# Head-norm sums from two rounded parts of the squares, and a rank-16 product with its weight parts side by side

## The chip, the cores and the metric

The kernel runs on one core of one Trainium2 chip. The metric is device time in microseconds from launch to end. A core has TensorE (PE: matrix products into PSUM; its weight loads are PEld), VectorE (DVE), ScalarE (ACT), GpSimd (POOL) and SyncE (SP), which issues most of the transfers. Each engine works through its own list in order; the lists are tied by semaphores only.

## The reference

One decoder layer on x (512 tokens, 1024 channels), float32: a gated feed-forward block, a mixing block, a second feed-forward block, a last norm. Only the mixing block matters here:

```python
proj = h @ w_in_mix          # hq hf hi hg | gq gk gv gg | g_low (16 columns) | r_hg r_gla
gk   = g_low @ w_gk_up + b_gk_up                       # rank 16 -> 256 decay logits
o    = chunked_gated_linear_attention(q, k, v, log_a)  # 4 HGRN2 heads, 4 GLA heads, 128 channels each
o    = rms_norm(o, norm_gain) * silu(g)                # per head: x * rsqrt(mean(x*x) + 1e-6) * gain
merged = sigmoid(r_hg) * (y_hg @ w_up_hg) + sigmoid(r_gla) * (y_gla @ w_up_gla)
```

## The kernel before

Activations lie with channels on the 128 partitions and the 512 tokens along the free axis. A large product is made from numbers in a rounded 32-bit format (fp32r), of which one pass of 512 columns goes through TensorE at a time. To keep float32 accuracy each operand is split into a high part (rounded) and a low part (the rest), and three passes are summed: high weight by high activation (L575), high by low (L576), low by high (L577). Weights come in units: 1024 rows by 256 columns in RAW; ScalarE writes the high part WH (L1127, `split_hi`), VectorE the low part WL (L1649, `split_lo`). Two slots alternate. The two "v" kinds are made the other way round, tokens out, in passes of 256 columns (L620 to L622).

The mixing block has 15 units, MIX: hf hq vh gh hf hq vh gh low gk gq vg gg vg gg, numbered 0 to 14. Unit 8, "low", has 16 columns. Each unit has 8 steps on TensorE, and the list STAGES_AT puts attention work between the steps: for each of 8 heads three groups of scores (`score_levels`, L898, L903, L904), the far scores (`score_far`, L913 to L921), the output (`head_out`, L934, into PSUM bank 7), and the norm sum (`head_norm`, L942). Head 0 has its norm at step 39, head 1 at 51, head 2 at 70 (inside "low", steps 64 to 71), head 3 at 89. The scores of head 1 start at step 41, of head 2 at 60, of head 3 at 78, of head 5 at 104.

ScalarE and VectorE follow one written list, ORDER: "... V0 A0 E3 a1 Q0 b1 T0 E4 U0 V1 A1 Q1 E5 T1 a2 U1 b2 E6 V2 A2 E7 Q2 a3 T2 b3 U2 E8 V3 G0 G1 A3 E9 Q3 a4 T3 E10 b4 ... E12 Q4 V5 A5 a5 ...". For a head or preparation j:

- E: ScalarE converts the next unit's high part and moves unit j out of PSUM; VectorE makes the next low part.
- a, b: decays and preparation of the score operands. VectorE runs a cumulative sum (L2092), GpSimd forms differences from it (L544 to L556), ScalarE takes exponentials, VectorE multiplies (L2114, L2115, L2120, L2123). The first scores of the head need the second L2123.
- V, A: VectorE and ScalarE copy scores out of PSUM (V: L2157, L2170).
- Q: ScalarE squares the head's output (L1522, in `squares`), one operation of 128x512 that raises sq_o; VectorE multiplies output by gate (L2176, in `gate_out`) and raises og_done. `head_norm` on TensorE waits for both and sums the squares over the 128 partitions with a matrix of ones, in float32.
- T, U: inverse root and gain (L1529, L1531, L2182), then high and low part of the result (L1535, L2186).

The rank-16 code is copied to S and multiplied by w_gk_up (GKW, 16 rows) in float32 (`gk_up`, L951, step 80).

Of the kernel before, what the change touches and what calls it, by code (L numbers as in the profile page):

```python
# [23 lines left out]
def trunk_program(nc, x, c, w_ada, b_ada, norm_gains, ffn1_w_in, ffn1_w_down, w_in_mix, w_gk_up, b_gk_up,  # L24
                  lb_logits, hg_norm, gla_norm, w_up_hg, w_up_gla, w_out, ffn2_w_in, ffn2_w_down,
                  final_norm, out):
    F32, F32R, BF16, I8 = mybir.dt.float32, mybir.dt.float32r, mybir.dt.bfloat16, mybir.dt.int8
    ACT, ALU = mybir.ActivationFunctionType, mybir.AluOpType
    ds = bass.ds

    P = 128
    T = x.shape[1]
    D = x.shape[2]
    DB = D // P
# [3 lines left out]
    CW = 256  # L38
# [3 lines left out]
    HEADS = 4  # L42
# [15 lines left out]
    N_MIX = N_F1DOWN + 11  # L58
# [7 lines left out]
    mix_at = {}  # L66
    for j, (kind, _, half) in enumerate(MIX):
        mix_at[kind, half] = j
    RANK = 16
# [3 lines left out]
    with ctx:  # L73
        def sb(name, shape, dt=F32):
            return ctx.enter_context(nc.sbuf_tensor(name, shape, dt))

        def sem(name):
            return ctx.enter_context(nc.semaphore(name))
# [5 lines left out]
        S = sb("S", [P, T])  # L84
# [18 lines left out]
        LBD = sb("LBD", [P, HEADS])  # L103
        GT = sb("GT", [P, 2, NC])
        FT = sb("FT", [P, 2, NC])
        GKW = sb("GKW", [RANK, 256])

        H_BYTES = DB * T * 4
        ARENA = 106496
# [3 lines left out]
        def place(name, shape, offset, dt=F32):  # L113
            return nc.alloc_sbuf_tensor_at(name, shape, dt, offset=base + offset)
# [54 lines left out]
        W512 = place("W512", [P, T], 104448)  # L169
        YH = [place("YHh", [P, HEADS, T], 8192, F32R), place("YHg", [P, HEADS, T], 0, F32R)]  # L170
        YL = [place("YLh", [P, HEADS, T], 16384, F32R), place("YLg", [P, HEADS, T], 24576, F32R)]
        MH = place("MH", [P, DB, T], 53248, F32R)
        ML = place("ML", [P, DB, T], 69632, F32R)
        RG = [place(f"RG{s}", [P, 2, T], 86016 + 4096 * s) for s in range(2)]
# [55 lines left out]
        near_done, evac_v = sem("near_done"), sem("evac_v")  # L230
        evac_a = sem("evac_a")
        pv_done = sem("pv_done")
        sq_o, og_done = sem("sq_o"), sem("og_done")
        n_done, rs_ln, rs_ready = sem("n_done"), sem("rs_ln"), sem("rs_ready")
        yf_ready, y_hi, y_lo = sem("yf_ready"), sem("y_hi"), sem("y_lo")

# [23 lines left out]
        def slot(n):  # L260
            return n % 2
# [27 lines left out]
        def norm_in(a):  # L289

            if a < HEADS:
                return CHG[:, a, :], KHG[:, a, :]
            return QHG[:, a - HEADS, :], VHG[:, a - HEADS, :]
# [50 lines left out]

        def ada_buffer(piece, j):
            return ADAW[1 if piece >= LATE_PIECE else 0][j]

        def mix_banks(j):
            return (2, 3) if j % 2 == 0 else (0, 1)
# [215 lines left out]
        def _(pe):  # L565
# [13 lines left out]
            def unit(n, value, banks, ahi, alo, kb0=0, nk=DB, first=True, last=True, wait_h=None,  # L579
                     width=CW, before=None):  # L580

                pe.wait_ge(unit_lo, value)
                whi, wlo = weights(n, width)
                for k in range(nk):
                    if before is not None:
                        before(k)
                    if wait_h is not None:
                        pe.wait_ge(h_lo, wait_h + k + 1)
                    for m in range(max(width // P, 1)):
                        w = slice(m * P, min((m + 1) * P, width))  # L590
                        rows = w.stop - w.start
                        ins = three(PS[0:rows, banks[m], :], whi[:, k, w], wlo[:, k, w], ahi[:, kb0 + k, :],
                                    alo[:, kb0 + k, :], first and k == 0, last and k == nk - 1)
                ins.then_inc(unit_done, 1)

            def unit_x(n, value, banks, ahi, alo, kb0=0, nk=DB, first=True, before=None):
# [13 lines left out]
            def unit_v(n, banks, before):  # L610

                pe.wait_ge(unit_lo, n + 1)
                whi, wlo = weights(n)
                for t in range(TT):
                    ps = PS[:, banks[t // 2], (t % 2) * CW:(t % 2 + 1) * CW]
                    tok = slice(t * P, (t + 1) * P)
                    for k in range(DB):
                        if k % 4 == 0:
                            before(2 * t + k // 4)
                        mm(ps, HH[:, k, tok], whi[:, k, :], start=k == 0, stop=False)  # L620
                        mm(ps, HL[:, k, tok], whi[:, k, :], start=False, stop=False)  # L621
                        ins = mm(ps, HH[:, k, tok], wlo[:, k, :], start=False, stop=k == DB - 1)  # L622
                ins.then_inc(unit_done, 1)
# [314 lines left out]
            def head_norm(a):  # L938

                pe.wait_ge(sq_o, a + 1)  # L940
                pe.wait_ge(og_done, a + 1)
                mm(PS[:, 7, :], ONES[:, :], norm_in(a)[0], start=True, stop=True).then_inc(n_done, 1)  # L942

            def gk_up():

                pe.wait_ge(gkw_in, 16)
                pe.wait_ge(mix_evac, mix_at["low", 0] + 1)
                pe.wait_ge(evac_a, 2 * HEADS - 3)
                pe.wait_ge(rs_ln, HEADS - 1)
                for g in range(2):  # L950
                    ins = mm(PS[:, 6 + g, :], GKW[:, g * P:(g + 1) * P], S[0:RANK, :], start=True, stop=True)  # L951
                ins.then_inc(gk_mm, 1)

            def stages_at(step):
# [24 lines left out]
            for j in range(2, len(MIX)):  # L979
                n = N_MIX + j  # L980
                kind = MIX[j][0]
                pe.wait_ge(mix_evac, j - 1)
                if kind in ("vh", "vg"):
                    unit_v(n, mix_banks(j), lambda k: stages_at(8 * j + k))
                else:
                    unit(n, n + 1, mix_banks(j), HH, HL, width=RANK if kind == "low" else CW, before=lambda k: stages_at(8 * j + k))


            def late_reduce(pair, b):
# [119 lines left out]
        def _(act):  # L1109
# [7 lines left out]

            for dst, src in small:
                act.dma_start(dst, src).then_inc(small_in, 16)
            act.dma_start(GKW[:, :], w_gk_up[0]).then_inc(gkw_in, 16)  # L1120

            def split_hi(n, raw_val, done_val=None, size=UNIT):

                act.wait_ge(raw_in[slot(n)], raw_val)
                if done_val is not None:
                    act.wait_ge(unit_done, done_val)
                A(WH[slot(n)][:, 0:size], RAW[slot(n)][:, 0:size], ACT.Copy).then_inc(unit_hi, 1)  # L1127

            def down_size(piece):
                return (UNIT, UNIT, (FB - 16) * CW)[piece]  # L1130
# [313 lines left out]
            def evacuate(j):  # L1444
                if MIX[j][0] in ("hf", "hq", "gh", "gg"):
                    tables[0] = "sigmoid or silu"
                n = N_MIX + j
                kind, _, half = MIX[j]
                act.wait_ge(unit_done, n + 1)
                ps = PS[:, mix_banks(j)[0]:mix_banks(j)[0] + 2, :]  # L1450
                two = slice(2 * half, 2 * half + 2)
                toks = ps.rearrange("p b (t c) -> p (b t) c", c=CW)
                if kind == "hf":
                    A(CHG[:, two, :], ps, ACT.Sigmoid)
                    A(KHG[:, two, :], ps, ACT.Sigmoid, scale=-1.0).then_inc(mix_evac, 1)
                elif kind == "hq":
                    A(QHG[:, two, :], ps, ACT.Silu).then_inc(mix_evac, 1)
                elif kind == "vh":
                    A(VHG[:, :, half * CW:(half + 1) * CW], toks, ACT.Copy).then_inc(mix_evac, 1)
                elif kind == "vg":  # L1460
                    A(VGL[:, :, half * CW:(half + 1) * CW], toks, ACT.Copy).then_inc(mix_evac, 1)
                elif kind == "gh":
                    A(GO[:, two, :], ps, ACT.Silu).then_inc(mix_evac, 1)
                elif kind == "gg":
                    A(GO[:, HEADS + 2 * half:HEADS + 2 * half + 2, :], ps, ACT.Silu).then_inc(mix_evac, 1)
                elif kind == "low":
                    A(S[0:RANK, :], PS[0:RANK, mix_banks(j)[0], :], ACT.Copy).then_inc(mix_evac, 1)
                elif kind == "gk":
                    A(KGL[:, :, :], ps, ACT.Copy).then_inc(mix_evac, 1)
                elif kind == "gq":  # L1470
                    A(QGL[:, :, :], ps, ACT.Copy, scale=64.0 ** -0.5).then_inc(mix_evac, 1)
# [47 lines left out]

            def squares(a):  # L1520
                act.wait_ge(pv_done, a + 1)
                A(norm_in(a)[0], PS[:, 7, :], ACT.Square).then_inc(sq_o, 1)  # L1522

            def inverse_rms(a):

# [107 lines left out]
        def _(dve):  # L1633
# [9 lines left out]
            def split_lo(n, value, done_val=None, size=UNIT):  # L1643

                if done_val is not None:
                    dve.wait_ge(unit_done, done_val)
                dve.wait_ge(unit_hi, value)
                s = slot(n)
                V.tensor_tensor(WL[s][:, 0:size], RAW[s][:, 0:size], WH[s][:, 0:size].bitcast(F32), ALU.subtract)\  # L1649
                    .then_inc(unit_lo, 1)  # L1650

# [520 lines left out]

            def gate_out(a):
                dve.wait_ge(sq_o, a + 1)
                dve.wait_ge(mix_evac, G_NEEDS[a])
                V.tensor_tensor(GO[:, a, :], GO[:, a, :], PS[:, 7, :], ALU.mult).then_inc(og_done, 1)  # L2176

# [172 lines left out]
```

## Time and profile before

| | |
|---|---|
| median of 3 runs | 1189.76 us (1188.7 to 1189.96) |
| profiled execution: its own time | 1188.77 us |
| its span, first to last instruction | 1186.9 us |
| granted TensorE clock, mean over the span | 0.992 |
| instructions | 18541 |
| DVE L1649 (low parts of weights) | 55 operations, 120.5 us |
| ACT L1127 (high parts of weights) | 55 operations, 100.5 us |
| DMA moved, mean | 143.51 MB, 121 GB/s |

Times in rows are microseconds from the span's start unless marked ns. A timeline row is start, duration, engine, line, operation, output<-input, shape, and in brackets the engine's idle time before it and what ended that. A matmul's shown duration includes its way through the pipeline, so the cost of one pass in a stream is read from start to start. PEclk is the granted clock as a share of full speed.

### The profile page before, as it was taken

What the parts mean: (1) busy time and instruction counts of PE and PEld (TensorE: products, weight loads), DVE (VectorE), ACT (ScalarE), POOL (GpSimd) and SP (SyncE); (2) the same over time, 40 slices, a digit from 0 to 9 for tenths busy, and PEclk for the clock granted to TensorE, in tenths of its full rate; (3) what the DMA queues carried; (4) which work ended last, traced back from release to release, by engine and by line L of the source; (5) the groups of instructions that cost most, each with busy time, mean ns of one, the idle gap of its engine ahead of it and who ended that gap; (6) DMA issues with size and microseconds to landing.
All of it is one profiled execution on the core that took longest, in us unless ns stands there. A gap on an engine that the chain in (4) does not pass through costs nothing.

```text
span 1186.9 us, 18541 instructions
## 1 busy us (share of the span) xinstructions
PE 1158.7 (98%) x7385; PEld 1039.3 (88%) x7385; DVE 781.7 (66%) x1061; ACT 507.5 (43%) x646; POOL 90.7 (8%) x137
## 2 busy tenths in 40 slices
PE   5999999999999999999999999999999999999997
PEld 5789999998889997877887888888999999998887
DVE  5788888767777677566463446755868887863222
ACT  6455554452222466555344322234455544452322
POOL 2000000002220122222010001000000000000000
PEclk8899999999999999999999999999999999999999
DMA  9433333337885131122221457442223333332211
GB/s 353 147 104 108 106 106 106 106 97 264 306 288 179 37 102 44 36 71 72 71 72 36 142 178 245 145 142 72 72 71 107 106 106 106 106 97 98 98 63 71
DMA packets 115126, 143.51 MB, mean 121 GB/s; under 512 B 4084, under 2 KB 102784, under 8 KB 115072
## 3 DMA queue, kind: packets, MB, share of 16 engines
q1 hardware_dynamic: 106800, 113.32, 29.2%
q0 software_dynamic: 8064, 29.36, 7.0%
q8 instruction: 37, 0.61, 0.2%
q14 instruction: 17, 0.14, 0.0%
q10 hardware_dynamic: 208, 0.08, 0.0%
HBM read 140.65 MB, written 2.10 MB: 120 GB/s over the span
## 4 chain that ended last, share of the span: by engine, by line
PE 87%; DVE 7%; ACT 4%; issue 1%; DMA 1%; SPq 0%; DVEq 0%; ACTq 0%
PE PS L819 29%; PE PS L575 16%; PE PS L577 15%; PE PS L576 15%; PE PS L898 1%; PE PS L934 1%; PE PS L620 1%; PE PS L904 1%; PE PS L621 1%; PE PS L622 1%; PE PS L733 1%; DVE ACC L1751 1%; DMA ADA<-in_w_ada_dram 1%; DVE ACC0a L1762 1%; ACT WH L1127 1%
## 5 line engine op out<-in xcount | busy, mean ns | idle before, releaser
L1649 DVE TENSOR_TENSOR WL<-RAW,WH 128x2048 fp32r<-128x2048 f32 (+2 forms) x55 | 120.5, 2191 | 129.4 <-ACT WH L1127 129.3
L575 PE MATMUL PS<-HH,WH 128*128 128x512 f32 (+2 forms) x488 | 186.1, 381 | 4.4 <-DVE HL L1677 3.0
L1127 ACT ACTIVATE WH<-RAW 128x2048 fp32r<-128x2048 f32 (+2 forms) x55 | 100.5, 1828 | 194.3 <-PE PS L577 187.7
L577 PE MATMUL PS<-HH,WL 128*128 128x512 f32 (+2 forms) x488 | 177.8, 364 | 0.0
L576 PE MATMUL PS<-HL,WH 128*128 128x512 f32 (+2 forms) x488 | 177.7, 364 | 0.0
L819 PE MATMUL PS<-HH,WH 128*128 128x256 f32 x576 | 163.3, 284 | 0.3
L819 PE MATMUL PS<-HL,WH 128*128 128x256 f32 x576 | 163.0, 283 | 0.0
L819 PE MATMUL PS<-HH,WL 128*128 128x256 f32 x576 | 163.0, 283 | 0.0
L575 PE MATMUL PS<-UH,WH 128*128 128x512 f32 (+1 forms) x416 | 147.0, 353 | 0.0
L577 PE MATMUL PS<-UH,WL 128*128 128x512 f32 (+1 forms) x416 | 145.8, 351 | 0.0
L576 PE MATMUL PS<-UL,WH 128*128 128x512 f32 (+1 forms) x416 | 145.8, 350 | 0.0
L819 PE MATMUL PS<-TH,WH 128*128 128x256 f32 x432 | 122.3, 283 | 0.0
L819 PE MATMUL PS<-TL,WH 128*128 128x256 f32 x432 | 122.3, 283 | 0.0
L819 PE MATMUL PS<-TH,WL 128*128 128x256 f32 x432 | 122.2, 283 | 0.0
L575 PEld LDWEIGHTS PS<-HH,WH 128*128 128x128 f32 (+1 forms) x488 | 91.9, 188 | 24.8 <-issue 6.7
L1930 DVE TENSOR_TENSOR WL<-SW,WH 128x1024 fp32r<-128x1024 f32 x72 | 88.2, 1225 | 35.3 <-ACT WH L1310 35.2
L819 PEld LDWEIGHTS PS<-HH,WH 128*128 128x128 f32 x576 | 110.5, 192 | 0.8 <-DVE WL L1936 0.7
L819 PEld LDWEIGHTS PS<-HL,WH 128*128 128x128 f32 x576 | 110.6, 192 | 0.1
L819 PEld LDWEIGHTS PS<-HH,WL 128*128 128x128 f32 x576 | 110.5, 192 | 0.0
L577 PEld LDWEIGHTS PS<-HH,WL 128*128 128x128 f32 (+1 forms) x488 | 92.0, 188 | 15.8
L576 PEld LDWEIGHTS PS<-HL,WH 128*128 128x128 f32 (+1 forms) x488 | 92.2, 189 | 14.3 <-issue 1.1
L1310 ACT ACTIVATE WH<-SW 128x1024 fp32r<-128x1024 f32 x72 | 76.2, 1058 | 66.7 <-PE PS L819 63.8
(320 smaller groups left out, 2244.3 us busy)
## 6 DMA issues: line engine op xcount, KB each, us to landing
RAW<-in_ffn_w_in_dram SPq DMA_DIRECT2D x42, 1024.0 KB, 5.1
ADAW<-in_w_ada_dram POOLq DMA_DIRECT2D x56, 512.0 KB, 5.6
RAW<-in_w_in_mix_dram SPq DMA_DIRECT2D x22, 1024.0 KB, 5.3
RAW<-in_ffn_w_down_dram SPq DMA_DIRECT2D x16, 1024.0 KB, 5.1
ADA<-in_w_ada_dram SPq DMA_DIRECT2D x16, 512.0 KB, 10.5
RAW<-in_ffn_w_down_dram SPq DMA_DIRECT2D x7, 768.0 KB, 4.5
RAW<-in_w_out_dram SPq DMA_DIRECT2D x3, 1024.0 KB, 5.1
XST<-in_x_dram SPq DMA_DIRECT2D x4, 512.0 KB, 5.3
```

The lines of the kernel that those rows point to most:

```text
L575: mm(ps, whi, ahi, start=start, stop=False)
L576: mm(ps, whi, alo, start=False, stop=False)
L577: return mm(ps, wlo, ahi, start=False, stop=stop)
L620: mm(ps, HH[:, k, tok], whi[:, k, :], start=k == 0, stop=False)
L621: mm(ps, HL[:, k, tok], whi[:, k, :], start=False, stop=False)
L622: ins = mm(ps, HH[:, k, tok], wlo[:, k, :], start=False, stop=k == DB - 1)
L733: ins = mm(PS[:, 6, m:m + 1], ACC[:, m * P:(m + 1) * P], ONES[:, 0:1], start=True, stop=True)
L819: ins = mm(PS[:, bank, ROW], wt, at_tokens[:, k, :], start=start and k == 0 and j == 0, stop=k == 3 and j == 2, skip_group_check=True)
L1127: A(WH[slot(n)][:, 0:size], RAW[slot(n)][:, 0:size], ACT.Copy).then_inc(unit_hi, 1)
L1310: A(WH[tile][:, 8 * P * (1 - j):8 * P * (2 - j)], SW[:, 2 * j:2 * j + 2, :].rearrange("p s c -> p (s c)"), ACT.Copy).then_inc(op_hi, 1)
L1649: V.tensor_tensor(WL[s][:, 0:size], RAW[s][:, 0:size], WH[s][:, 0:size].bitcast(F32), ALU.subtract)\
L1930: V.tensor_tensor(WL[tile][:, w], SW[:, 2 * j:2 * j + 2, :].rearrange("p s c -> p (s c)"), WH[tile][:, w].bitcast(F32), ALU.subtract).then ...
```

## The change

The squares of each head are written twice by ScalarE, once in full and once rounded (SQH). VectorE subtracts to get the low part (SQL), ahead of the gate product. TensorE sums both rounded parts with the ones read as fp32r: two fp32r passes where there was one float32 product. SQL of the HGRN2 heads overwrites the full squares in place.

For unit "low" the two weight parts (16 columns each) lie side by side in WH, so that one pass multiplies both: 8 steps with two passes each (all 32 weight columns by HH, then by HL) in place of 8 with three. The 32 output rows go to S, and GKW holds w_gk_up twice, one copy below the other, so that `gk_up` adds the two halves.

```diff
-        GKW = sb("GKW", [RANK, 256])
+        GKW = sb("GKW", [2 * RANK, 256])
+        SQH = [place("SQHh", [P, HEADS, T], 16384, F32R), place("SQHg", [P, HEADS, T], 0, F32R)]
+        SQL = [place("SQLh", [P, HEADS, T], 8192, F32R), place("SQLg", [P, HEADS, T], 24576, F32R)]
...
+        def side_by_side(n):
+            both = WH[slot(n)][:, 0:2 * DB * RANK].rearrange("p (k c) -> p k c", c=2 * RANK)
+            return both[:, :, 0:RANK], both[:, :, RANK:2 * RANK], both
...
+            def low_unit(n, bank, before):
+                pe.wait_ge(unit_lo, n + 1)
+                both = side_by_side(n)[2]
+                for k in range(DB):
+                    before(k)
+                    mm(PS[0:2 * RANK, bank, :], both[:, k, :], HH[:, k, :], start=k == 0, stop=False)
+                    ins = mm(PS[0:2 * RANK, bank, :], both[:, k, :], HL[:, k, :], start=False, stop=k == DB - 1)
+                ins.then_inc(unit_done, 1)
...
             def head_norm(a):
                 pe.wait_ge(sq_o, a + 1)
+                pe.wait_ge(sq_lo, a + 1)
                 pe.wait_ge(og_done, a + 1)
-                mm(PS[:, 7, :], ONES[:, :], norm_in(a)[0], start=True, stop=True).then_inc(n_done, 1)
+                ones = ONES[:, :].bitcast(F32R)
+                mm(PS[:, 7, :], ones, SQH[a // HEADS][:, a % HEADS, :], start=True, stop=False)
+                mm(PS[:, 7, :], ones, SQL[a // HEADS][:, a % HEADS, :], start=False, stop=True).then_inc(n_done, 1)
...
-                pe.wait_ge(gkw_in, 16)
+                pe.wait_ge(gkw_in, 32)
...
-                    ins = mm(PS[:, 6 + g, :], GKW[:, g * P:(g + 1) * P], S[0:RANK, :], start=True, stop=True)
+                    ins = mm(PS[:, 6 + g, :], GKW[:, g * P:(g + 1) * P], S[0:2 * RANK, :], start=True, stop=True)
...
-            act.dma_start(GKW[:, :], w_gk_up[0]).then_inc(gkw_in, 16)
+            for part in range(2):
+                act.dma_start(GKW[RANK * part:RANK * (part + 1), :], w_gk_up[0]).then_inc(gkw_in, 16)
...
-                    A(S[0:RANK, :], PS[0:RANK, mix_banks(j)[0], :], ACT.Copy).then_inc(mix_evac, 1)
+                    A(S[0:2 * RANK, :], PS[0:2 * RANK, mix_banks(j)[0], :], ACT.Copy).then_inc(mix_evac, 1)
...
             def squares(a):
                 act.wait_ge(pv_done, a + 1)
-                A(norm_in(a)[0], PS[:, 7, :], ACT.Square).then_inc(sq_o, 1)
+                A(norm_in(a)[1], PS[:, 7, :], ACT.Square)
+                A(SQH[a // HEADS][:, a % HEADS, :], PS[:, 7, :], ACT.Square).then_inc(sq_o, 1)
...
             def gate_out(a):
                 dve.wait_ge(sq_o, a + 1)
+                V.tensor_tensor(SQL[a // HEADS][:, a % HEADS, :], norm_in(a)[1], SQH[a // HEADS][:, a % HEADS, :].bitcast(F32),
+                                ALU.subtract).then_inc(sq_lo, 1)
                 dve.wait_ge(mix_evac, G_NEEDS[a])
                 V.tensor_tensor(GO[:, a, :], GO[:, a, :], PS[:, 7, :], ALU.mult).then_inc(og_done, 1)
```

`split_hi` and `split_lo` of unit "low" write the two halves of `side_by_side`, 128 values per partition each as before.

## Rows read from the trace of the kernel before

**Rows 1.** the page: busy time by engine; the chain that ended last.

```profile
PE 1158.7 (98%) x7385; PEld 1039.3 (88%) x7385; DVE 781.7 (66%) x1061; ACT 507.5 (43%) x646; POOL 90.7 (8%) x137
...
PE 87%; DVE 7%; ACT 4%; issue 1%; DMA 1%; SPq 0%; DVEq 0%; ACTq 0%
```

**Rows 2.** windows: stretch, its us, PE PEld DVE ACT POOL busy, PEclk, DMA, GB/s.

```profile
440.00:670.00 230.00, 227.74 (x1237) 182.01 (x1236) 130.53 (x232) 111.70 (x156) 34.88 (x44) 1.00 0.22 69
40.00:54.00 14.00, 13.13 (x54) 10.41 (x54) 7.82 (x12) 5.59 (x7) 0.00 (x0) 0.76 0.46 152
```

**Rows 3.** waits of TensorE, mixing stage: total us, times, longest.

```profile
PE PS L898 <- DVE KP L2123: 1.0, 3, 0.6
PE PS L951 <- issue: 0.6, 1, 0.6
PE PS L942 <- DVE GO L2176: 0.5, 1, 0.5
```

**Rows 4.** groups, mixing stage: count | busy us, mean ns | idle before.

```profile
L575 PE MATMUL PS<-HH,WH 128*16 128x512 f32 x8 | 3.6, 456 | 0.0
```

**Rows 5.** timeline, TensorE, around head 2: start, duration (us), instruction, count.

```profile
519.28 1.02 PE L942 MATMUL PS<-CHG,ONES 128*128 128x512 f32 x2
...
520.36 0.40 PE L576 MATMUL PS<-HL,WH 128*16 128x512 f32 x1
...
521.06 0.39 PE L576 MATMUL PS<-HL,WH 128*16 128x512 f32 x1
```

**Rows 6.** timeline, all engines, around head 0.

```profile
459.75 0.69 DVE L2176 TENSOR_TENSOR GO<-GO,PS 128x512 f32<-128x512 f32 x1 [0.77 <-ACT CHG L1522]
...
460.36 0.87 DVE L2114 TENSOR_TENSOR QU<-QU,QHG 128x512 f32<-128x512 f32 x1
...
460.59 1.10 PE L942 MATMUL PS<-CHG,ONES 128*128 128x512 f32 x2 [0.48 <-DVE GO L2176]
460.64 1.48 POOL L553 TENSOR_TENSOR KP<-CHG 128x512 f32<-128x512 f32 x1
...
461.15 1.52 DVE L2115 TENSOR_TENSOR KL<-KL,KHG 128x512 f32<-128x512 f32 x1
...
464.14 0.41 DVE L2123 TENSOR_TENSOR KP<-KP,KHG 128x256 f32<-128x256 f32 x1
...
464.61 0.55 PE L898 MATMUL PS<-QP,KP 128*128 128x64 f32 x3 [0.18 <-DVE KP L2123]
```

**Rows 7.** timeline, ScalarE, around head 1.

```profile
482.85 0.60 ACT L1522 ACTIVATE CHG<-PS 128x512 f32<-128x512 f32 x1 [4.32 <-PE PS L934]
483.34 1.91 ACT L1127 ACTIVATE WH<-RAW 128x2048 fp32r<-128x2048 f32 x1
```

**Rows 8.** timeline, ScalarE and VectorE, around head 2.

```profile
517.35 0.59 ACT L1522 ACTIVATE CHG<-PS 128x512 f32<-128x512 f32 x1
...
517.97 0.69 DVE L2176 TENSOR_TENSOR GO<-GO,PS 128x512 f32<-128x512 f32 x1 [0.46 <-ACT CHG L1522]
...
520.10 1.23 DVE L2092 TENSOR_TENSOR_SCAN CHG<-RST,CHG 128x512 f32<-128x512 bf16 x1 [1.04 <-ACT CHG L1483]
```

**Rows 9.** timeline, VectorE and TensorE, head 4.

```profile
593.25 0.69 DVE L2176 TENSOR_TENSOR GO<-GO,PS 128x512 f32<-128x512 f32 x1 [0.46 <-ACT QHG L1522]
593.85 0.91 DVE L2157 COPY_PREDICATED SC<-MASK,PS 128x256 f32<-128x256 int8 x2
...
594.91 0.29 PE L903 MATMUL PS<-QP,KP 64*128 64x64 f32 x1
```

**Rows 10.** timeline, VectorE and TensorE, heads 3 and 7.

```profile
553.33 0.69 DVE L2176 TENSOR_TENSOR GO<-GO,PS 128x512 f32<-128x512 f32 x1 [0.71 <-ACT CHG L1522]
...
556.68 1.02 PE L942 MATMUL PS<-CHG,ONES 128*128 128x512 f32 x2
...
655.48 0.68 DVE L2176 TENSOR_TENSOR GO<-GO,PS 128x512 f32<-128x512 f32 x1
...
657.27 0.59 PE L942 MATMUL PS<-QHG,ONES 128*128 128x512 f32 x1
```

More of the change, by code:

```diff
@@ L232, in trunk_program @@
         pv_done = sem("pv_done")
-        sq_o, og_done = sem("sq_o"), sem("og_done")
+        sq_o, sq_lo, og_done = sem("sq_o"), sem("sq_lo"), sem("og_done")
         n_done, rs_ln, rs_ready = sem("n_done"), sem("rs_ln"), sem("rs_ready")
@@ L984, in _ @@
                     unit_v(n, mix_banks(j), lambda k: stages_at(8 * j + k))
+                elif kind == "low":
+                    low_unit(n, mix_banks(j)[0], lambda k: stages_at(8 * j + k))
                 else:
-                    unit(n, n + 1, mix_banks(j), HH, HL, width=RANK if kind == "low" else CW, before=lambda k: stages_at(8 * j + k))
+                    unit(n, n + 1, mix_banks(j), HH, HL, before=lambda k: stages_at(8 * j + k))
             def late_reduce(pair, b):
@@ L1126, in split_hi @@
                     act.wait_ge(unit_done, done_val)
-                A(WH[slot(n)][:, 0:size], RAW[slot(n)][:, 0:size], ACT.Copy).then_inc(unit_hi, 1)
+                if n == N_MIX + mix_at["low", 0]:
+                    A(side_by_side(n)[0], RAW[slot(n)][:, 0:size].rearrange("p (k c) -> p k c", c=RANK), ACT.Copy).then_inc(unit_hi, 1)
+                else:
+                    A(WH[slot(n)][:, 0:size], RAW[slot(n)][:, 0:size], ACT.Copy).then_inc(unit_hi, 1)
             def down_size(piece):
@@ L1648, in split_lo @@
                 s = slot(n)
+                if n == N_MIX + mix_at["low", 0]:
+                    hi, lo, _ = side_by_side(n)
+                    V.tensor_tensor(lo, RAW[s][:, 0:size].rearrange("p (k c) -> p k c", c=RANK), hi.bitcast(F32), ALU.subtract)\
+                        .then_inc(unit_lo, 1)
+                    return
                 V.tensor_tensor(WL[s][:, 0:size], RAW[s][:, 0:size], WH[s][:, 0:size].bitcast(F32), ALU.subtract)\
```

## The prediction

> **What bounds the kernel now.** I read the page first, for the busy shares and the chain that ended last: TensorE is busy for 98% of the span and carries 87% of the chain [rows 1]. Then the windows: in the mixing stage, 440 to 670 us, TensorE is busy 227.7 of 230 us at full clock, with VectorE at 130.5 and ScalarE at 111.7 [rows 2]. So a pass less on TensorE looks like time gained. But the change also lengthens the way over ScalarE and VectorE, and TensorE does wait for that way in a few places. So I read the waits of TensorE next [rows 3]: three times for the score operands (1.0 us in all), once 0.6 ahead of L951 (there the unit's low part is due, an L1649 that VectorE makes after the same score operands), once 0.5 for the gate product of a head. Each is small, but a wait above zero marks a place where TensorE is early: what TensorE saves ahead of it is lost in the wait, and what VectorE or ScalarE adds ahead of it is paid in full. So the sum is made piece by piece between these places, from the timelines.
>
> **What TensorE saves.** The float32 sum of a head is two passes [rows 5]. It starts at 519.28; the third matmul behind it (the second L576) starts at 521.06, four matmuls after its end, at a pace of (521.06 - 520.36)/3 = 0.233 each. So the sum costs 521.06 - 519.28 - 4 x 0.233 = 0.85 us. Two fp32r passes at 0.23 cost 0.46. Saved: 0.39 a head, 8 x 0.39 = 3.1 us. Unit "low" has 8 passes of each kind [rows 4], 24; 16 remain. A pass of 16 weight columns costs the same 0.233 as any [rows 5], so 32 columns cost no more: 8 x 0.233 = 1.9 us saved. Together 5.0 us, if all of it counted.
>
> **What ScalarE and VectorE add, per head.** One more square: 0.59 long, but the operation behind a square starts 0.49 after it [rows 7], so +0.5 on ScalarE, and sq_o rises 0.5 later. One more subtraction SQL on VectorE ahead of the gate product. No row shows it; its bounds are the gate product, same shape, 0.69 with a start-to-start of 0.61, and L2115, two SBUF inputs beside a GpSimd operation, 1.52 [rows 6]. GpSimd works at head 0 only (in the other pieces SQL falls into its pauses), so I take 0.6 start to start elsewhere. A head's gate product then ends 0.5 + 0.6 = 1.1 later.
>
> **Head 0.** The square ended at 459.73, GO ran 459.75 to 460.44, and TensorE, which had waited 0.48 us, started at 460.59, 0.15 after it [rows 6]. New: squares to 460.23; SQL ends by about 461.2 (nearest row: L2114 at 460.36, same shape and inputs, 0.87, beside the same GpSimd work); GO to 461.85; norm sum from 462.0, +1.4. It is 0.39 shorter, so TensorE goes on at +1.0. Before, it came to the next scores (L898, 464.61) with 0.18 idle; its last matmul had started at 464.04 by the modelled length of 0.39, so it could have started at 464.27. New: 465.3. VectorE's second L2123 ended at 464.55; it too moves, but less than GO, since L2115 now falls mostly behind GpSimd's work: about 465.2. TensorE is late by 465.3 - 464.6 = **+0.7**. With SQL at 0.69 it is +0.4, at 1.52 +1.2.
>
> The Trainium skill, "SBUF — State Buffer", section "Who interferes with whom", says that a VectorE operation with two SBUF inputs and a GpSimd operation that reads SBUF exclude each other for the whole instruction, and that one with a single SBUF input is free. The rows bear it out: GO, which reads PSUM, ran in 0.69 beside GpSimd, and L2115 ended just after L553 (462.12) by the time of one operation [rows 6]. By that rule SQL waits for the GpSimd operation under way and then blocks the next: +0.8 for the piece. Without the rule it would be +0.4.
>
> **Head 1.** The square (482.85, for which ScalarE had waited 4.32 us) stands directly ahead of the conversion L1127 [rows 7], of E5, T1, a2 and so of everything up to the scores of head 2 at step 60, where TensorE waits (one of the three waits in [rows 3]). +0.5 on ScalarE passes through. SQL is hidden: VectorE has nothing to do until the conversion of 1.91 us ends. TensorE's 0.39 at step 51 lies ahead of that wait and is lost. **+0.5**, bounds 0.4 and 0.6.
>
> **Head 2.** The same, towards the scores of head 3 at step 78. The squares begin at 517.35; VectorE's sum L2092 starts at 520.10 after an idle 1.04 behind the decay logarithm L1483 of ScalarE [rows 8]. SQL takes 0.6 more on VectorE against that idle 1.04, so only ScalarE's 0.5 counts: **+0.5** (0.4 to 0.6). At this norm TensorE waits for GO: 518.66 + 1.1 + 0.15 = 519.9, while it is there from 519.28 less six steps of "low" at one pass less, 1.4. Then it runs to step 78, and would be there early. It waits. So the 0.39 and the whole 1.9 us of unit "low" are lost: the waits at L898 and L951 [rows 3] only grow.
>
> **Heads 3 and 7.** At head 3 GO ends at 554.02 and TensorE comes at 556.68; at head 7 655.48 + 0.68 = 656.16 against 657.27 [rows 10]. A GO later by 1.1 is just in time in both; at head 7 SQL may start as soon as L1649 is through, so it is +0.6 there. Heads 4, 5 and 6 do not wait either (L942 waited once in eight [rows 3]). So each of heads 3 to 7 keeps its saving: 5 x 0.39 = **-2.0 us**; if one loses it, -1.6.
>
> **Head 4, the new place.** Behind its GO (593.25 to 593.94) VectorE runs the two L2157 of head 5's scores (593.85, 0.91 long), and 0.15 after them, at 594.91, TensorE starts L903 of the third group, which reuses their bank [rows 9]. That is a chain without slack: square + 0.5, SQL + 0.6. **+1.1** (0.6 to 1.3).
>
> **Edits at nothing.** The second w_gk_up transfer is one more issue on ScalarE's queue at the very start, beside a TensorE that waits for others; 32 rows in place of 16 for L951 and the copy to S change no column count. Strided conversions of "low" handle the same 128 values. If the cover went, each is some tenths.
>
> **Sum.** +0.7 + 0.5 + 0.5 + 1.1 - 2.0 = +0.8, with the 0.1 by the rule left aside. On the profiled execution (span 1186.9, 1188.77 in all) that is 1189.6; the median of the runs shown stands 0.99 above it, so 1190.6 in those terms. With all low bounds 0.4 + 0.4 + 0.4 + 0.6 - 2.0 = -0.2, with all high ones 1.2 + 0.6 + 0.6 + 1.3 - 1.6 = +2.1: the forecast's own range is 1189.6 to 1191.9. Below 0.2% (2.4 us) a measurement of this kernel does not tell a change from none, so the forecast is "same".
>
> **Rivals.**
>
> 1. The savings count. If the waits in [rows 3] are no more than jitter of an engine that is busy 98% [rows 1], the 5.0 us come through: 1184.7, faster. For it: 2.3 us idle in 230 [rows 2]. Against it: the idle stands where the lists cross, with a named releaser. Half-way, if ScalarE's 0.5 hides at heads 1 and 2 but the savings there still die, it is 1189.8, still same. Chance of the faster case 0.14.
> 2. SQL in front of the preparation. If SQL isn't hidden at heads 1 and 2, and at head 3, whose GO stands directly ahead of the next cumulative sum (L2092), reaches the scores of head 4, then 1.2 + 1.1 + 1.1 + 1.1 + 1.1 - 2.0 = +3.6: 1193.4, slower. It decides once the pieces add up to over 4.4 us against the 2.0 saved. Against it: the idle 1.04 in [rows 8] and the conversion of 1.91 in [rows 7]. Chance 0.09.
> 3. The clock. Near the start, 40 to 54 us, where TensorE had waited, the granted clock averaged 0.76 [rows 2], that is part of the time at 1.2 in place of 2.4 GHz, which cost 0.24 x 14 = 3.4 us. At head 0 the wait grows from 0.5 to 1.9 us. If the clock falls there: 1190.6 + 3.4 = 1194.0, slower. Against it: 1.00 throughout the stage, waits of 0.6 included. Chance 0.04.
> 4. It doesn't do what it says: a pass with the ones read as fp32r costs as much as a float32 one. Then the 2.0 are gone and head 0 pays 0.4 more: +3.2, 1193.0, slower. Against it: the same format in L576 at 0.233. Chance 0.05.
>
> **Chances.** The forecast 0.68, rival 1 0.14, rivals 2 to 4 0.18 together. Faster by over 0.2% 0.14; within 0.2% 0.69 (the forecast and the weak ends of the rivals); slower 0.17. Eight times in ten: 1187.0 to 1193.2.
>
> **What would show it.** L942 as two passes 0.23 apart, x16 in all. A wait of about 1.9 us at head 0's norm; the waits at L898 for heads 2 and 3 not smaller but larger, together by over 2 us; a new wait of about 1.3 us ahead of L903 in the third group of head 5; no wait at the norms of heads 3 to 7. L2092 of head 3 later against the end of unit 7 by 0.5. I am wrong if the wait at L898 for head 3 stays at its old size while unit "low" is 1.9 shorter (rival 1), if SQL shows over 1 us outside head 0 or delays an L2092 of heads 1 to 3 by more than 0.6 (rival 2), or if PEclk is below 1.00 anywhere in the stage (rival 3).

## The result

| | kernel before | changed kernel |
|---|---|---|
| median (runs) | 1189.64 us (17) | 1190.96 us (17) |
| lowest to highest | 1187.42 to 1190.22 | 1189.55 to 1192.37 |
| ratio, after to before | | 1.0016 (95% interval 1.0009 to 1.0024) |
| profiled execution, span | 1186.9 us | 1189.5 us |

The forecast was 1190.6, no change that can be told. The median is 0.4 us above it and inside the range; the time is longer by 0.16%, with an interval that reaches both sides of the 0.2% below which I called two times the same. The way there was as forecast in most of its waits and wrong in one term, the clock.

### The profile page after: what moved, and what is told of

Same layout as the page of the kernel before. It is cut to its first block, busy times and chain, and to the rows that moved or that the text cites. A ratio compares the mean times of both kernels' runs of the same rounds, so it can differ in the third digit from the quotient of the medians.

```text
span 1189.5 us, 18534 instructions
## 1 busy us (share of the span) xinstructions
PE 1156.6 (97%) x7377; PEld 1041.4 (88%) x7377; DVE 785.7 (66%) x1069; ACT 511.5 (43%) x654; POOL 90.5 (8%) x137
## 4 chain that ended last, share of the span: by engine, by line
PE 87%; DVE 6%; ACT 4%; issue 1%; DMA 0%; ACTq 0%; DVEq 0%
PE PS L836 29%; PE PS L582 16%; PE PS L584 16%; PE PS L583 16%; PE PS L915 1%; PE PS L951 1%; PE PS L921 1%; PE PS L637 1%; PE PS L638 1%; PE PS L639 1%; PE PS L750 1%; DVE ACC L1783 1%; ACT WH L1153 1%; PE PS L938 1%; DVE ACC0b L1794 1%
## 5 line engine op out<-in xcount | busy, mean ns | idle before, releaser
L1681 DVE TENSOR_TENSOR WL<-RAW,WH 128x2048 fp32r<-128x2048 f32 (+1 forms) x54 | 120.2, 2226 | 128.2 <-ACT WH L1153 128.1
L582 PE MATMUL PS<-HH,WH 128*128 128x512 f32 (+1 forms) x480 | 182.5, 380 | 4.5 <-DVE HL L1709 3.0
L1153 ACT ACTIVATE WH<-RAW 128x2048 fp32r<-128x2048 f32 (+1 forms) x54 | 100.2, 1856 | 194.5 <-PE PS L584 187.7
L584 PE MATMUL PS<-HH,WL 128*128 128x512 f32 (+1 forms) x480 | 175.6, 366 | 0.0
L583 PE MATMUL PS<-HL,WH 128*128 128x512 f32 (+1 forms) x480 | 175.6, 366 | 0.0
L582 PEld LDWEIGHTS PS<-HH,WH 128*128 128x128 f32 x480 | 92.0, 192 | 23.5 <-issue 5.8
L836 PEld LDWEIGHTS PS<-HH,WH 128*128 128x128 f32 x576 | 110.5, 192 | 0.8 <-DVE WL L1968 0.7
L836 PEld LDWEIGHTS PS<-HL,WH 128*128 128x128 f32 x576 | 110.6, 192 | 0.1
L836 PEld LDWEIGHTS PS<-HH,WL 128*128 128x128 f32 x576 | 110.6, 192 | 0.0
L584 PEld LDWEIGHTS PS<-HH,WL 128*128 128x128 f32 x480 | 91.9, 191 | 15.0
L583 PEld LDWEIGHTS PS<-HL,WH 128*128 128x128 f32 x480 | 92.2, 192 | 12.9
```

Source lines behind the costliest of these rows:

```text
L582: mm(ps, whi, ahi, start=start, stop=False)
L583: mm(ps, whi, alo, start=False, stop=False)
L584: return mm(ps, wlo, ahi, start=False, stop=stop)
L836: ins = mm(PS[:, bank, ROW], wt, at_tokens[:, k, :], start=start and k == 0 and j == 0, stop=k == 3 and j == 2, skip_group_check=True)
```

## The profile after

The page of the changed kernel, the line that answers to the busy times in [rows 1]:

```profile
PE 1156.6 (97%) x7377; PEld 1041.4 (88%) x7377; DVE 785.7 (66%) x1069; ACT 511.5 (43%) x654; POOL 90.5 (8%) x137
```

Eight passes fewer, eight VectorE and eight ScalarE operations more. TensorE is 2.1 us less busy in a span that is 2.6 us longer: the saving is there and stands as idle time. It is less than the 5.0 us of passes because passes at a lower clock, shown below, are busy for longer. Its waits in the mixing stage, changed kernel; they answer to [rows 3] (L961 is the first pass of the head norm, L915 the first score group, L920 the later ones, L971 the rank-16 up-projection). The two waits of L961 are at heads 0 and 2, the one of L915 is at the scores of head 2, the one of L920 at head 5's third group:

```profile
PE PS L961 <- DVE GO L2210: 3.7, 2, 1.9
PE PS L915 <- DVE KP L2155: 1.4, 1, 1.4
PE PS L920 <- DVE SC L2189: 1.1, 1, 1.1
PE PS L971 <- issue: 0.3, 1, 0.3
```

Head 0 in the changed kernel, timeline, answering to [rows 6] (L1548 and L1549 are the two squares, L2207 is the subtraction SQL, L2210 the gate product):

```profile
459.29 1.75 POOL L557 TENSOR_TENSOR KP<-CHG 128x256 f32<-128x256 f32 x3
...
459.50 0.58 ACT L1548 ACTIVATE KHG<-PS 128x512 f32<-128x512 f32 x1
...
459.98 0.59 ACT L1549 ACTIVATE SQHh<-PS 128x512 fp32r<-128x512 f32 x1
...
460.60 0.99 DVE L2207 TENSOR_TENSOR SQLh<-KHG,SQHh 128x512 fp32r<-128x512 f32 x1 [1.25 <-ACT SQHh L1549]
461.01 1.48 POOL L560 TENSOR_TENSOR KP<-CHG 128x512 f32<-128x512 f32 x1
...
461.52 0.67 DVE L2210 TENSOR_TENSOR GO<-GO,PS 128x512 f32<-128x512 f32 x1
...
462.34 0.52 PE L961 MATMUL PS<-SQHh,ONES 128*128 128x512 f32 x1 [1.86 <-DVE GO L2210]
```

The second square starts 0.48 after the first, SQL lasts 0.99 beside GpSimd, and the gate product 0.67: each term of head 0 has about the size that the forecast gave it. But look at TensorE's pace right behind it, in the same execution:

```profile
463.08 0.63 PE L582 MATMUL PS<-HH,WH 128*128 128x512 f32 x1
463.51 0.63 PE L583 MATMUL PS<-HL,WH 128*128 128x512 f32 x1
...
466.29 0.40 PE L584 MATMUL PS<-HH,WL 128*128 128x512 f32 x1
466.52 0.40 PE L582 MATMUL PS<-HH,WH 128*128 128x512 f32 x1
```

First 0.43 from start to start, then 0.23. The clock was at its lower level (1.2 GHz) for a while behind the wait of 1.86 us. Windows of the changed kernel, columns as in [rows 2], PEclk the third number from the end:

```profile
460.00:470.00 10.00, 8.14 (x38) 6.54 (x37) 9.40 (x21) 9.02 (x14) 3.63 (x4) 0.83 0.00 0
520.00:530.00 10.00, 8.16 (x29) 5.74 (x28) 6.94 (x12) 7.44 (x13) 5.12 (x8) 0.83 0.34 107
440.00:670.00 230.00, 223.40 (x1219) 182.00 (x1219) 132.83 (x240) 115.05 (x164) 34.84 (x44) 0.99 0.21 65
```

**Where the time went.** For every matmul that both kernels have I took its start in the changed kernel less its start in the profile of before. That lag is constant while TensorE works at its pace and steps where something differs. The table gives the step of each piece; the start-up (to 50 us) differs between any two executions, also of one kernel, and is apart. It is worked out from the traces' start times (`after` is the first profile of the changed kernel; after_b and after_c are two more profiles of the changed kernel, see below).

```
step of the lag, us        forecast   after  after_b  after_c
start-up, to 50 us             -      +0.33   +1.13    +1.47
head 0                       +0.7     +2.13   +0.60    +0.60
head 1 -> scores of head 2   +0.5     +0.48   +0.49    +0.49
head 2 -> up-projection      +0.5     +0.48   +1.40    +1.40
head 4 -> scores of head 5   +1.1     +1.07   +1.07    +1.07
norms of heads 3 to 7        -2.0     -1.90   -1.89    -1.91
mixing stage in all          +0.8     +2.26   +1.67    +1.65
```

In each profile four of five terms hit to 0.1 us. What stands above the forecast, 0.9 to 1.5 us, is one stretch at the lower clock, at head 0 or behind the scores of head 3. The first profile has a second stretch, at 524 us, that cost nothing: it took up idle time, and no wait is left at the scores of head 3.

## The experiments

**One part alone: the rank-16 unit.** The head norms go back to one square and one float32 product (`low_only`):

```diff
-                pe.wait_ge(sq_lo, a + 1)
-                mm(PS[:, 7, :], ones, SQH[a // HEADS][:, a % HEADS, :], start=True, stop=False)
-                mm(PS[:, 7, :], ones, SQL[a // HEADS][:, a % HEADS, :], start=False, stop=True).then_inc(n_done, 1)
+                mm(PS[:, 7, :], ONES[:, :], norm_in(a)[0], start=True, stop=True).then_inc(n_done, 1)
```

> Only the rank-16 unit is changed: 16 passes for 24, head norms as before. Theory (the saving lies ahead of the wait for head 3's scores and dies in it): TensorE reaches step 78 some 1.9 us early and waits, so the wait at L898 of head 3 (0.3 us idle before) grows to about 2.1 us and the wait ahead of the rank-16 up-projection stays; time within 0.3 us of before. Rival (passes saved are time saved): 1.9 us faster than before, ratio 0.9984, and the wait at head 3's scores no larger.

Measured: ratio 1.0001 (0.9992 to 1.001). The lag falls by 1.14 us to the last pass that both kernels have ahead of head 2's norm (+0.35 to -0.79) and is back at +0.35 when the scores of head 3 start; at the end it is +0.36. The wait there, timeline of this kernel (L917 is the first score group):

```profile
530.54 1.66 PE L917 MATMUL PS<-QP,KP 128*128 128x64 f32 x13 [1.19 <-DVE KP L2164]
```

Idle rises from 0.3 to 1.19 there, and 0.7 of the saving goes already in a wait at head 2's norm, since TensorE now comes there earlier than ScalarE and VectorE. The wait ahead of the up-projection stays at 0.6, as expected. The expectation's 2.1 was wrong in its place, not in its sum: two waits took the saving. The unit's saving does not reach the end.

**The other part alone: the head norms.** `norm_only`, the rank-16 unit as before:

```diff
-                elif kind == "low":
-                    low_unit(n, mix_banks(j)[0], lambda k: stages_at(8 * j + k))
```

> Only the head norms are changed, the rank-16 unit has its 24 passes. Theory: the same as the whole change within 0.4 us, that is 1 to 2.7 us slower than before (0.8 by the waits, up to 1.6 more where the clock falls at head 0), since the rank-16 unit's saving never reached the end. TensorE's wait at head 2's norm is shorter than the 1.9 us of the whole change by the 1.4 us that six steps of a third pass take, about 0.5, so the clock stays at full speed there. Rival (the saving counted): 1.9 us slower than the whole change.

Measured: 1.0021 (1.0011 to 1.003), median 1190.99, as the whole change. Steps: head 0 +2.13 with a stretch at the lower clock, head 1 +0.48, head 2 to the up-projection +0.50, head 4 +1.08. A second stretch fell behind the up-projection, at 543 us, and cost 1.5. TensorE's wait at head 2's norm is 0.5, as expected; that the clock would hold behind it was wrong by that second stretch. As far as the intervals tell, the whole of the change's cost is in the norms.

**Only where nobody waits.** The new sum in heads 3, 5, 6 and 7 (`late_heads`):

```diff
+        SPLIT = (3, 5, 6, 7)
+                if a not in SPLIT:
+                    A(norm_in(a)[0], PS[:, 7, :], ACT.Square).then_inc(sq_o, 1)
+                    return
```

> The new sum only in heads 3, 5, 6 and 7; heads 0, 1, 2 and 4 keep the float32 sum with one square and no subtraction; the rank-16 unit is changed. Theory: the heads whose squares stand ahead of a wait of TensorE pay, the others keep 0.39 us each, so 4 x 0.39 = 1.6 us faster than before (ratio 0.9987), no wait at the norm of head 0 over 0.5 us, no fall of the clock in the stage, and no wait ahead of head 5's third group of scores. Rival (the second square and the subtraction cost wherever they stand): no faster than before.

Measured: 0.999 (0.9981 to 0.9999), medians 1188.17 and 1188.9: faster, though by less than the 0.9987 expected, and the interval ends just below 1. In the lag: 0.02 or less at heads 0, 1, 2 and 4, and -0.40 directly at each of the four norms, -1.5 in all. Clock 1.00 through the stage. One part of the expectation missed: a norm does wait, head 2's, 0.7 us, for the reason just given.

**The norms later in TensorE's list.** Head 0's at step 42, head 2's at 73 (`later_norms`):

```diff
-        STAGES_AT = [(29, 30, 31, 32, 34, 39), ..., (60, 61, 62, 63, 65, 70),
+        STAGES_AT = [(29, 30, 31, 32, 34, 42), ..., (60, 61, 62, 63, 65, 73),
```

> The whole change, with the norm of head 0 at step 42 for 39 and of head 2 at step 73 for 70, so that TensorE finds both operands there. Theory: the two waits of 1.9 us ahead of the norms are gone (under 0.3 each) and with them the half-speed stretches of 3.4 us, so granted clock 1.00 from 440 to 670 us; TensorE then waits at the scores of head 1 instead, for VectorE, which is 0.6 late. Time 0.4 to 0.9 us above before in every run, without the group of runs near 1192. Rival (the half-speed stretch has another cause than the wait): it is still there, and the time is that of the whole change.

Measured: 1.0094 (1.0079 to 1.0109), over 10 us slower: a miss. ScalarE's list, this kernel's timeline (L1556 is the first step of the inverse root, and L962 is the second pass of head 0's norm sum):

```profile
473.11 0.69 ACT L1556 ACTIVATE KHG<-PS,EPST 128x512 f32<-128x512 f32 x1 [7.87 <-PE PS L962]
```

I had asked what the norm waits for, not who waits for the norm. T0 (the inverse root) stands in ScalarE's list ahead of E4, and VectorE's V1 behind E4; head 1's later score groups waited for those in turn, so that the three lists waited for one another in a ring. The lag jumps from +2.5 to +8.6 there. The lower clock came too, at 466 us and at 541 us.

**One step later.** Head 0's norm at step 40, head 2's at 71 (`one_step_later`), so that six passes run in the wait and the norm starts when it did.

```diff
+        STAGES_AT = [(29, 30, 31, 32, 34, 40), ..., (60, 61, 62, 63, 65, 71),
```

> The whole change with the norm of head 0 at step 40 for 39 and of head 2 at step 71 for 70: six passes (1.37 us) run in what was a wait of 1.9 us, and the norm itself starts when it did, unlike the kernel with the norms three steps later, where ScalarE and VectorE then stood waiting for the sum. Theory: waits at the norms of 0.5 us, granted clock 1.00 in 440 to 670 us, scores of head 1 at +0.7; in all 0.6 us above before and 1.3 below the whole change on average. Rival (the half-speed stretch has another cause): still there, time as the whole change.

Measured: 1.0019 (1.0006 to 1.0031). Windows of this kernel, around head 0 and behind head 3's scores:

```profile
455.00:475.00 20.00, 18.33 (x95) 15.17 (x93) 17.54 (x34) 12.84 (x20) 6.68 (x8) 1.00 0.18 54
530.00:548.00 18.00, 16.55 (x75) 12.66 (x73) 13.55 (x30) 6.52 (x9) 0.00 (x0) 0.91 0.19 58
```

Head 0 costs +0.61 at full clock, and TensorE now waits 1.16 us for VectorE at the scores of head 1. The wait at head 2's norm is 1.38, where I had expected 0.5. And the stretch at the lower clock came at 534.1 us, behind the waits at head 2's norm and head 3's scores, and cost what it had cost elsewhere. Waiting was moved, not removed: the kernel still idles TensorE, and the clock still fell. My expectation of 1.00 throughout was wrong.

**The second square alone**, in the kernel before (`square_only`); its result is read by nobody:

```diff
+                A(norm_in(a)[1], PS[:, 7, :], ACT.Square)
                 A(norm_in(a)[0], PS[:, 7, :], ACT.Square).then_inc(sq_o, 1)
```

> The kernel before with one more square per head on ScalarE, ahead of the one that is used; its result is written where the next operation overwrites it and is read by nobody. No subtraction, float32 sums, rank-16 unit as before. Theory: 0.5 us passes through at heads 0 (0.3 to 0.5), 1, 2 and 4, nothing at the others, so 1.8 us slower (ratio 1.0015), and TensorE's start of the scores of heads 2 and 3 is 0.5 us later each, that of head 5's third group 0.5 later. Rival (an engine 43% busy has room): within 0.3 us of before.

Measured: 1.0033 (1.0022 to 1.0043), 3.9 us, twice what I expected. The steps in its profile: head 0 +0.15, head 1 +0.48, head 2 +0.47, head 4 +0.48, sum 1.6; and +1.56 at 541 us from the lower clock. So the square passes as forecast through three places, costs little at head 0, and the rest is the clock again: 1.58 + 1.56 = 3.1 of the 3.9. At head 0 the norm moves by 0.5, but by the prediction's estimate TensorE could have started the next scores at 464.27 and started at 464.61, so 0.34 of it falls into that slack.

**The subtraction alone** (`sub_only`):

```diff
                 dve.wait_ge(sq_o, a + 1)
+                V.tensor_tensor(norm_in(a)[1], norm_in(a)[0], norm_in(a)[0], ALU.subtract)
```

> The kernel before with one more subtraction of 128x512 per head on VectorE ahead of the gate product (the squares minus themselves, read by nobody). One square, float32 sums. Theory: 0.5 to 1.0 us at head 0, where GpSimd works beside it, 0.6 at head 4, nothing at heads 1, 2, 3, 5, 6, 7: 1.1 to 1.6 us slower (ratio 1.001). At heads 1 and 2 the starts of the next scores don't move. Rival (hidden nowhere): 0.6 also at heads 1 and 2, 2.3 to 2.8 us slower.

Measured: 1.0012 (1.0001 to 1.0023). Steps: head 0 +0.62, head 4 +0.59, all others 0.02 or less. It hides at heads 1 and 2, as the idle times had said. No stretch at the lower clock here, though TensorE waits 1.3 us at head 0's norm.

**A version that uses it** (`best2`): the new sum in heads 3 to 7, the rank-16 unit changed, and two exchanges in ORDER.

```diff
+        SPLIT = (3, 4, 5, 6, 7)
-        ORDER = "... a3 T2 b3 U2 E8 ... E12 Q4 V5 A5 ..."
+        ORDER = "... a3 T2 b3 E8 U2 ... E12 V5 Q4 A5 ..."
```

> The new sum in heads 3 to 7 only, rank-16 unit changed, and two places of the order changed: at head 4 the copies of head 5's scores stand ahead of the gate product (V5 Q4 for Q4 V5), and after head 3's preparation the low part of unit 10 stands ahead of head 2's result (E8 U2 for U2 E8). Theory: 5 x 0.39 saved by the sums, 0.2 at head 5's third group, 0.6 ahead of the rank-16 up-projection: 2.8 us faster than before (ratio 0.9977) and 1.2 faster than late_heads, with no wait ahead of the up-projection over 0.2 us. Rival (order changes only move the waits): as late_heads, 1.6 us faster than before.

Measured: 0.9976 (0.9966 to 0.9987), median 1186.6 us against 1189.09 of the kernel before beside it: faster than the kernel before, by what was forecast (0.9977), and, going by the two ratios to it, than the changed kernel. Its waits and its stage:

```profile
PE PS L917 <- DVE KP L2164: 1.9, 3, 1.2
PE PS L964 <- DVE GO L2220: 1.2, 2, 0.8
...
440.00:670.00 230.00, 226.77 (x1240) 183.50 (x1240) 132.00 (x236) 114.21 (x161) 34.91 (x44) 1.00 0.23 74
```

The wait ahead of the up-projection is gone (step -0.59) and so is the one at head 5's third group (-0.10, where I had written 0.2); the five norms give -1.9 together. The step of -0.59 belongs to the exchange E8 U2, since `late_heads` has the same rank-16 unit and no step there. All in all -2.6 in the stage. It did not get faster through the rank-16 unit, whose saving still ends in the 1.2 us wait at head 3's scores.

**More profiles of both kernels**, one execution each.

> The whole change again, one more profile. Theory (the wait of 1.9 us at head 0 brings the clock down, but only where it falls right): the piece at head 0 costs either about 2.1 us with a half-speed stretch of 3.4 us or about 0.7 without. Rival (the fall is fixed by the program): the same stretches at the same places as in the first profile.

> As the run before it; a third profile of the whole change. The waits at the norms of heads 0 and 2 are 1.9 us within 0.1 in each.

> The kernel before again, one more profile. Theory: no half-speed stretch between 440 and 670 us, and the start-up (to 50 us) differs by up to 2 us between executions, which makes the two groups of times that the runs of every kernel show.

> As the run before it: a third profile of the kernel before, again without a half-speed stretch in the mixing stage by the theory.

Windows of after_b, and then of before_b:

```profile
460.00:470.00 10.00, 8.14 (x44) 6.60 (x43) 8.74 (x21) 8.98 (x15) 4.39 (x6) 1.00 0.00 0
533.00:540.00 7.00, 7.00 (x35) 6.23 (x36) 6.96 (x15) 1.11 (x2) 0.00 (x0) 0.76 0.00 0
```

```profile
440.00:670.00 230.00, 227.75 (x1236) 182.07 (x1236) 130.54 (x232) 111.66 (x156) 34.86 (x44) 1.00 0.22 69
```

The three profiles of the changed kernel have the same wait of 1.86 us at head 0, to the hundredth. In one the clock falls behind it, in two it doesn't and falls at 535 us instead, so the place moves from one execution to the next, as expected; that it falls elsewhere was not foreseen. In none of three profiles of before does it fall in the stage. A stretch that cost time came in three of three. The start-up differs by 1.1 us between the three of before and by 1.1 us between the three of after, which is as wide as much of what was to be measured here.

## Why the prediction was right, and where it was not

1. What bounds it: right. The 5.0 us of passes did not come through; TensorE's busy time fell and its idle time grew.
2. TensorE's savings: right in size (0.38 each against 0.39 at heads 3 to 7) and in which of them count: five norms, none of the rank-16 unit (`low_only`). Not right was that the wait ahead of the up-projection, L951, would grow with the unit's saving: it stays at 0.6 in `low_only`.
3. Head 0: the mechanism and its terms right. +0.60 against +0.7 where the clock holds (after_b and after_c; +0.61 in `one_step_later`). Less the lag of 0.37 that the first profile has ahead of head 0, SQL ended at 461.22, GO at 461.82 and the sum started at 461.97, where I had written 461.2, 461.85 and 462.0. Two paths arrive at the next scores together: in after_b TensorE's last pass starts 0.22 ahead of them and VectorE's second L2155 ends 0.09 ahead. In `one_step_later` TensorE came 1.16 us early and the scores were as late, so moving the norm one step in TensorE's list frees TensorE and leaves VectorE's 0.6. The reading that SQL stands behind the GpSimd operation under way was right too: 0.99 long, between 0.69 and 1.52. The words that GpSimd works at head 0 only were not: it works at other heads too, but outside the time of SQL. By the rule of the Trainium skill's page "SBUF — State Buffer", "Who interferes with whom", it is to end by one operation's time after the one under way: L557 ended at 461.04, SQL at 461.59. This trace agrees, and at the other heads, where GpSimd pauses, SQL is 0.69. The whole piece came out at 0.60, between the 0.8 that I had worked out with the rule and the 0.4 without.
4. Heads 1 and 2: right, +0.48 each, ScalarE's half only (`square_only` +0.48, `sub_only` 0.00). At head 2 VectorE's subtraction used up half of the idle: 0.45 left ahead of the cumulative sum (L2092, L2124 in the changed kernel), where there had been 1.04 [rows 8].
5. Heads 3 and 7 lose nothing: right. Head 4: right, +1.07 for +1.1, half from the square and half from the subtraction, 0.48 and 0.59 by the two kernels that hold one each.
6. Rival 3, the clock, is the step that failed. I gave it 0.04, arguing from 1.00 throughout a stage whose waits were 0.6 at most, while the change makes them 1.9. It came in every profile of the changed kernel. Its price was also off: 3.4 us from a stretch near the start [rows 2], against 0.9 to 1.6 here, since the stretches were shorter and a part may fall into a wait that TensorE had anyway: in after_b and after_c the 0.6 ahead of the up-projection, at head 2 in the first profile all of it.
7. The signs that were named. Seen: 1.86 us at head 0's norm, 1.1 ahead of the third group of head 5, none at the norms of heads 3 to 7, SQL at 0.69 outside head 0. Not seen: waits at the scores of heads 2 and 3 larger together by over 2 us. They were 0.55 + 0.30, and became 1.42 + 0.97 in after_b, since 1.8 us went first in the wait at head 2's norm, which the prediction had worked out and left out of this sign. And the sign of being wrong by rival 3, a PEclk below 1.00 in the stage, came.

That the median agrees within 0.4 us is in part luck. 0.8 for the waits and 0.9 to 1.5 for the clock would make 1.7 to 2.3 in the stage, and the medians of 17 runs differ by 1.3; the start-up's spread of over 1 us lies in both.

**Open.** Whether the two groups of times of the changed kernel (seven runs from 1189.55 to 1189.75, ten from 1190.61 to 1192.37) are executions without and with such a stretch was not tried: three profiles all had at least one, at 1191.37, 1191.55 and 1191.92, and none is from the lower group. The mean clocks of the runs don't decide it: five of the lower seven have 0.994, as `square_only` has in its profiled run with one stretch. Nor is it shown that the kernel before never has one: of its 62 runs beside the experiments five took 1191.3 us or more, and none of these was profiled. What exactly brings the clock down stays open as well: 1.86 us of wait at head 0 did in one of three (and in `norm_only`), 1.3 us in `sub_only` did not, and `square_only` had its stretch with no wait over 1.0. That the longer waits bring it is argued from where it came, not shown.

## What to carry to other kernels

Count a saved pass only if no wait of its engine lies between it and the end of the stage, and an added operation in full if it stands ahead of such a wait: the lag of one engine's instructions between two traces shows both at a glance. A precision trick that trades TensorE passes for work on ScalarE and VectorE belongs where these two run ahead, not everywhere; here in five heads of eight, worth 1.9 us; two exchanges of neighbours in the order brought the other 0.7 of the 2.6. And before lengthening a wait on TensorE past those that the trace shows, price what a stretch at the lower clock would cost.

## What was not expected of the hardware

- The granted clock dropped to half for a few microseconds, in a stage where TensorE is 97% busy. The matmul pace in it is 0.43 us in place of 0.23. It fell at 463 to 467, 524, 534 to 535 or 541 to 543 us, by kernel and execution.
- A second square of a PSUM bank on ScalarE costs 0.48 us, not its shown 0.59: the next operation starts before the shown end.
- The first 50 us, where all these kernels do the same but for one small transfer, differ by up to 3.0 us between executions (lags of -1.3 to +1.7 against the profile of before); from there to 440 us the lag moves by less than 0.1 us.
